# The sample's threshold search as a seventh column of the prompt's search, in a two-layer decoder trunk

## The reference, cut to what matters

```python
sc = indexer_scores(iqb, iwb, ik)                   # relu(iq . ik), weighted over 8 index heads
sc = jnp.where(adm[None], sc, -jnp.inf)             # only admissible keys
_, idx = lax.top_k(sc, topk)                        # topk = 256
valid = idx <= qpos[None, :, None]
return attend_selected(qb, k[bi, idx], v[bi, idx], valid)
```

## Time and profile before

| what | value |
|---|---|
| median of 3 runs | 2226.55 us (2226.4 to 2228.27) |
| time of the profiled execution | 2228.04 us |
| its span, first to last instruction | 2226.3 us |
| mean granted TensorE clock | 0.933 of full speed |
| busy: TensorE, VectorE, ScalarE, GpSimd | 2014.0, 1001.8, 685.4, 599.0 us |
| first Q unit's rotation starts | 1359.60 us |
| attention over the prompt starts on VectorE | 1580.09 us |
| the prompt's counts (L1394, 6 areas x 31 bits) | 175.9 us |

### The profile page before, as it was taken

How to read it: one execution, slowest core, us unless ns; L and a number is a source line. 1 busy time by engine, 2 the same in 40 slices (tenths; PEclk the granted TensorE clock), 3 DMA queues, 4 the chain that set the end, 5 groups by cost and what they waited for, 6 DMA issues and landing times. The chain is left out here.

```text
span 2226.3 us, 33761 instructions
## 1 busy us (share of the span) xinstructions
PE 2014.0 (90%) x12572; PEld 1815.4 (82%) x12572; DVE 1001.8 (45%) x1842; ACT 685.4 (31%) x929; POOL 599.0 (27%) x321
## 2 busy tenths in 40 slices
PE   7999998999999999996898788989878987879998
PEld 6999998999999999995853478989655655569898
DVE  3123333111234421425578667779889821230533
ACT  4243332122433322322464211222444522120310
POOL 4333333553334356352110011112101100025221
PEclk8999999999999999997988788989999987689999
DMA  5222222222222232211301202112300014341021
GB/s 166 76 67 77 74 75 75 66 85 85 77 84 84 85 85 79 77 35 49 117 12 35 67 20 78 28 48 95 99 1 1 1 36 152 121 148 47 29 69 40
DMA packets 240515, 152.87 MB, mean 69 GB/s; under 512 B 24946, under 2 KB 235634, under 8 KB 240050
## 3 DMA queue, kind: packets, MB, share of 16 engines
q1 hardware_dynamic: 229314, 140.74, 21.3%
q10 hardware_dynamic: 10192, 9.46, 1.3%
q0 software_dynamic: 928, 1.62, 0.3%
HBM read 135.33 MB, written 16.43 MB: 68 GB/s over the span
## 5 line engine op out<-in xcount | busy, mean ns | idle before, releaser
L392 POOL TENSOR_TENSOR wlo<-wraw,whi 128x1024 fp32r<-128x1024 f32 x177 | 430.1, 2430 | 951.6 <-ACT whi L387 949.9
L404 PE MATMUL PS<-hhi_g,whi 128*128 128x288 f32 (+1 forms) x1536 | 328.2, 295 | 14.4 <-POOL wlo L392 10.8
L404 PE MATMUL PS<-hhi_g,wlo 128*128 128x288 f32 (+1 forms) x1536 | 321.3, 291 | 0.0
L404 PE MATMUL PS<-hlo_g,whi 128*128 128x288 f32 (+1 forms) x1536 | 321.0, 291 | 0.0
L404 PE MATMUL PS<-hhi,whi 128*128 128x364 f32 x1176 | 275.2, 344 | 48.7 <-POOL wlo L392 13.9
L387 ACT ACTIVATE whi<-wraw 128x1024 fp32r<-128x1024 f32 x177 | 186.6, 1055 | 357.7 <-PE PS L404 311.6
L404 PE MATMUL PS<-hlo,whi 128*128 128x364 f32 x1176 | 268.0, 337 | 0.0
L404 PE MATMUL PS<-hhi,wlo 128*128 128x364 f32 x1176 | 265.9, 335 | 0.0
L404 PEld LDWEIGHTS PS<-hhi,whi 128*128 128x128 f32 x1176 | 211.6, 197 | 57.7 <-issue 35.5
L404 PEld LDWEIGHTS PS<-hhi_g,whi 128*128 128x128 f32 x1536 | 243.5, 191 | 17.8 <-issue 10.7
L404 PEld LDWEIGHTS PS<-hlo_g,whi 128*128 128x128 f32 x1536 | 245.1, 191 | 0.0
(11 more groups left out here) (331 smaller groups left out, 2773.3 us busy)
## 6 DMA issues: line engine op xcount, KB each, us to landing
wraw<-in_w_in_a_dram SPq DMA_DIRECT2D x96, 512.0 KB, 3.9
wraw<-in_w_out_a_dram SPq DMA_DIRECT2D x32, 512.0 KB, 4.1
wraw<-in_w_in_b_dram SPq DMA_DIRECT2D x25, 512.0 KB, 3.7
wraw<-in_w_pe_gate_dram SPq DMA_DIRECT2D x16, 512.0 KB, 4.1
kpg<-in_cache_k_dram SPq DMA_DIRECT2D x64, 128.0 KB, 2.0
vpg<-in_cache_v_dram SPq DMA_DIRECT2D x64, 128.0 KB, 2.0
xs<-xT SPq DMA_DIRECT2D x1, 4368.0 KB, 12.6
xT<-xs SPq DMA_DIRECT2D x1, 4368.0 KB, 13.3
```

The lines of the kernel that those rows point to most:

```text
L392: nc.gpsimd.tensor_tensor(wlo[par][:], wraw[par][:], whi[par][:].bitcast(F32), ALU.subtract).then_inc(w_lo, 1)
L404: mm = nc.tensor.matmul(o, w[par][:, k, :], r(k, c0, cn), start=first and i == 0 and n == 0, stop=last and i == KD - 1 and n == 2)
```

## The change

The sample's first 19 bits (JOINT = 31 - 8 - 4) are taken together with the prompt's, from the first Q unit on: eight in the Q units and eleven after them. A joint bit has seven areas and seven columns, on 128 rows; `count` takes its number of rows from each area, so the sample's count still runs on 64 rows. Four memsets give rows 64 to 127 of column 6 defined values. The sample's last 12 bits stay in attention, in iterations 32 to 43 (SIDE = 32), and its resolve parts move to iterations 44 to 51.

```diff
@@ -332,7 +332,8 @@
         xs_out, xs_in, tabI, tabQ, pt_in = (sem(n) for n in ("xs_out", "xs_in", "tabI", "tabQ", "pt_in"))
 
         BITS, EARLY_BITS, KV_BITS = 31, 8, 2 * NKV
-        SIDE = 25
+        JOINT = BITS - EARLY_BITS - KV_BITS
+        SIDE = 32
 
 
         iq = {n: sem(f"iq_{n}") for n in ("swa", "t1d", "add")}
@@ -1386,11 +1387,13 @@
 
             PROMPT = (P, slice(0, NBLK - 2), [sc[:, block_off(b):block_off(b + 1)] for b in range(2, NBLK)])
             SAMPLE = (NS, slice(NBLK - 2, NBLK - 1), [scs[:]])
+            BOTH = (P, slice(0, NBLK - 1), PROMPT[2] + SAMPLE[2])
 
             def count(group, op, against):
 
-                rows, cols, areas = group
+                _, cols, areas = group
                 for j, x in enumerate(areas, cols.start):
+                    rows = x.shape[0]
                     own.link(nc.vector.tensor_scalar(acc[0:rows, 0:x.shape[1]], x,
                                                      0.0 if against is None else against[0:rows, j:j + 1], None,
                                                      op, ALU.add, accum_out=cnt[0:rows, j:j + 1]))
@@ -1417,12 +1420,13 @@
                 own.link(nc.vector.tensor_tensor(tbit[r, c], tbit[r, c], mbit[r, c], ALU.bitwise_xor))
                 own.link(nc.vector.tensor_scalar(bitc[r, c], bitc[r, c], 1, None, ALU.logical_shift_right))
 
-            BIT_LINKS = 5 + len(PROMPT[2])
-
-            def search_bits(trips):
+            def bit_links(group):
+                return 5 + len(group[2])
+
+            def search_bits(group, trips):
                 with dve.Fori(0, trips) as i:
-                    own.enter(i, BIT_LINKS)
-                    search_bit(PROMPT)
+                    own.enter(i, bit_links(group))
+                    search_bit(group)
                 own.leave(trips)
 
 
@@ -1453,7 +1457,7 @@
 
             dve.wait_ge(sc_ok, NBLK - 2)
             start_search(PROMPT)
-            search_bits(EARLY_BITS)
+            search_bits(PROMPT, EARLY_BITS)
             dve.wait_ge(ss_["sum"], DEC_B)
             nc.vector.tensor_copy(scs[:], PSF[0:NS, 0:SLS]).then_inc(ss_["cp"], 1)
 
@@ -1480,19 +1484,21 @@
 
 
             dve.wait_ge(ss_["ok"], 1)
+            for t, fill in ((tbit, 0), (bitc, 0), (sgn, 1.0), (cnt, 0.0)):
+                own.link(nc.vector.memset(t[NS:P, NBLK - 2:NBLK - 1], fill))
             start_search(SAMPLE)
 
 
             dve.wait_ge(kk_["st"], 16 * 6)
             with dve.Fori(0, NH // 2) as i:
-                own.enter(i, 2 + 2 * BIT_LINKS)
+                own.enter(i, 2 + 2 * bit_links(BOTH))
                 for ff in range(2):
                     f = 2 * i + ff
                     rotate(qq, U_Q + f, f, (U_Q + ff) % 2, qT[:, bass.ds(f, 1), :].rearrange("p o n -> p (o n)"),
                            csQ, snQ, gqk[:, 0:1])
-                    search_bit(PROMPT)
+                    search_bit(BOTH)
             own.leave(NH // 2)
-            search_bits(BITS - EARLY_BITS - KV_BITS - NH)
+            search_bits(BOTH, JOINT - NH)
             for rows, j in ((NS, slice(0, 1)), (P, slice(1, 9))):
                 dve.wait_ge(qq["rt"], 2)
                 own.link(nc.vector.reciprocal(qs[0:rows, j, :], qs[0:rows, j, :]))
@@ -1562,10 +1568,10 @@
                         resolve(PROMPT, b - 2, sc[:, block_off(b):block_off(b + 1)], kTb[:, 0], kTb[:, 1], part)
                 if n == NH:
                     sample_operands()
-                if SIDE <= n < SIDE + BITS:
+                if SIDE <= n < SIDE + BITS - JOINT:
                     search_bit(SAMPLE)
-                elif n >= SIDE + BITS:
-                    resolve(SAMPLE, NBLK - 2, scs[:], Ps, acc, n - SIDE - BITS)
+                elif SIDE + BITS - JOINT <= n < SIDE + BITS - JOINT + 8:
+                    resolve(SAMPLE, NBLK - 2, scs[:], Ps, acc, n - SIDE - BITS + JOINT)
                 if n + 2 < len(STEPS):
                     mask_and_max(n + 2)
             inverse_sums(NGR - 1)
```

## The result

The changed kernel takes 2235.88 us (median of 5 runs, 2235.04 to 2239.62) against 2226.55 of the kernel before. The ratio is 1.0041 with a 95% interval of 1.0028 to 1.0053. The profiled execution took 2235.04 us with a span of 2233.3.

A forecast was written before the change was run, and what follows sets the result against it. VectorE's order was taken to bound the kernel ahead of attention, with VectorE and TensorE close bounds in attention. 26.2 - 10.3 - 6.0 = +9.9 us on the 2226.55 median gave 2236.4 us, range 2230.0 to 2243.0.

The forecast's parts named there:

- VectorE's order is the chain from the first Q unit to attention: Q and Z units: VectorE has no slack, arrives last at attention by some 2 us, so added counts delay attention fully.
- The term: Ahead of attention: 19 added sample counts of 1.38 us each, 26.2 us in all, range 22 to 30.
- The five small instructions with a seventh column and the memsets cost nothing: Joint bits and before the first tq: seventh column priced at nothing, four memsets hidden in 5.24 us of waiting.
- The Z units move by 9.7 us, and TensorE then stands idle some 20: Ahead of attention: Z units move 7 x 1.38 = 9.7 us, the last ends near 1584, TensorE idles some 20 us.
- First stretch: Attention iterations 26 to 31, which lose their bits: step 33's maximum at 1641.0 instead of 1651.29, 10.3 us gained.
- Second stretch: Attention iterations 32 to 43: twelve bits as before, VectorE bound, same pace, nothing gained or lost.
- Third stretch: Attention iterations 44 to 53, no bits: TensorE alone needs 36.5 us instead of 42.5, 6.0 us gained.
- The sum: Whole kernel: 26.2 - 10.3 - 6.0 = +9.9 us, 2236.4 us against the median.
- TensorE not the next bound: Rival, attention iterations 26 to 31 and 44 to 53: all 43.7 us come back, -17.5 us, 2209; chance 0.06.
- The counts hidden ahead of attention: Rival, Q rounds and Z units: slack on VectorE hides the joint counts, leaving -16.3 us, 2210; chance 0.04.
- Less coming back because of the clock: Rival, attention's third stretch: TensorE's clock at the lower level, stretch gives nothing, +15.9 us, 2242.5; chance 0.12.
- The count at the plain rate: Rival, joint bits: added counts run at the plain comparison's rate, 15.4 us added, -0.9 in sum, 2225.6; chance 0.02.

The follow-up runs named there:

- e4_joint_q: Changed kernel with 8 joint bits (Q units) instead of 19, the other 23 in attention iterations 32 to 54: 2230.53 us, ratio 1.0000 to the kernel before.
- e5_gap: Changed kernel with the Q units' 8 sample bits as separate bits in the wait for ScalarE's swap, 11 joint bits kept: 2225.73 us, ratio 0.9993.
- e9_balance: Changed kernel without joint bits or memsets: sample bits in VectorE's waits and attention, two prompt bits moved ahead of K and V: 2192.84 us, ratio 0.9826.
- e2_no_side: Changed kernel without the 12 sample bits of attention iterations 32 to 43, resolve parts kept: 2224.62 us, ratio 0.9979 to the kernel before.
- e1_two_counts: Changed kernel with the sample's count issued twice in each of its 19 joint bits: 2263.57 us, ratio 1.0139 to the kernel before.
- e8_plain: Changed kernel with the sample's count in the 19 joint bits as a plain comparison without accumulator: 2229.75 us, ratio 0.9992.

## Why the prediction was right, point by point

**VectorE's order is the chain from the first Q unit to attention.** Right, and shown by four runs: the added counts (+25.8 us), doubled (another +24.1), eleven of them taken out (e4_joint_q, -12.2) and eight (e5_gap, -10.0). The term was 26.2. The short instructions that the splits stretched took 6.3 us extra before and 5.5 after, so without that chance the term would have measured 26.6. The prediction's "by some 2 us" was too large a lead: it set the end of the last bit against attention's start, with six small instructions between them, and the first maximum also waits for the store of the last Z unit, which by the estimate at e9_balance had landed only some 0.85 us earlier. With work added to VectorE this changed nothing.

**The five small instructions with a seventh column and the memsets cost nothing.** In the Q rounds each of the five takes 0.15 or 0.17 us, on seven columns as on six, and the first tq still waits 4.41 us for TensorE behind the memsets, where it waited 5.24. A round grew by 1.46 us (10.21 over seven), 0.08 more than the 1.38 of a count; where these 0.6 us in all come from no run shows.

**The Z units move by 9.7 us, and TensorE then stands idle some 20.** The last Z unit came at 1583.60 (forecast near 1584), the idle time was 19.83 us.

**First stretch, -10.3.** Measured -10.8.

**Second stretch, no change.** 54.42 against 54.41 us: VectorE's pace, untouched.

**Third stretch, -6.0.** This term was mis-sized: it measured -7.3. TensorE needed 35.10 us from iteration 45 to 54, not 36.5, because the waits of 0.35 us in even iterations, which I had carried over from the stage with bits, are gone: in iteration 46 above the transposes follow 1.50 us after the logits began, and seven blocks of logits at 0.215 are 1.51. To attention's end the stretch gave 18.1 - 10.8 = 7.3.

**The sum.** 25.8 - 18.1 = +7.7 us in these two stages, against +9.9. The two measured ratios give 6 to 12 and 5 to 9 us. That the median came within 0.5 us of the forecast is luck: the return was 1.8 us larger than its term and the added part 0.4 smaller, and the rest of the program, which the change leaves alone, varies by more than that from one execution to the next.

**The rivals.** TensorE not the next bound: out by e2_no_side, where 27.6 us less of VectorE's work gave 13.6. The counts hidden ahead of attention: out by e1_two_counts. Less coming back because of the clock: the 20 us of idle time ahead of attention changed nothing, attention's first 5 us are at 0.50 (the 1.2 GHz level) in both kernels, and steps 0 to 26 keep their distances to within 0.5 us. The third stretch, where this rival saw the lower level, ran at 0.99 (1719.70 to 1760.00). The count at the plain rate: out. The existing counts run at 1337 ns, and e8_plain shows that it is the accumulator that makes the difference. The Trainium skill, "VectorE: DVE Perf Modes", section "The perf-mode tier table (the rule you actually need)", has fp32 tensor_scalar at two elements a cycle: the trace agrees for the plain form (779 ns) and not for the one with a sum (1337 ns).

## What to carry to other kernels

When work is moved out of a stage, price it twice: at what it costs where it goes (all of it, if that engine's own order is the chain there), and at what comes back where it leaves (only down to the next engine's time, here 18.1 of 43.7 us). Before widening an instruction chain that is already the critical one, look inside it for waits on another engine: a whole bit of 2.3 us fitted into a wait of 3.5 us and cost nothing, where one more column of 1.38 us cost all of itself. And among stages with two close bounds put movable work where the other engine's steps are longest, and not in every step.

## What the runs showed of the hardware that was not expected

A plain fp32 comparison on VectorE (64x1088) took 779 ns alone, and up to 2596 ns when GpSimd's subtraction of 128x1024 was running; the same pass with an accumulated sum took 1337 ns and was not held up in the kernel after or in e1_two_counts. The short instructions on six or seven columns were held up too: two to four times in the Z units, by 3.7 to 8.4 us in all. That chance meeting was most of the difference between expected and measured stages in e4_joint_q, e5_gap and e8_plain. The Trainium skill, "GPSIMD Engine Reference", section "1. Specifications", says that GpSimd's SBUF interfaces are shared with VectorE and that instructions in a two-port mode or with two SBUF inputs contend; the trace agrees for the plain comparison and for the small ones, most of which have two inputs (mbit, tbit, cand, thr); in the kernel before one with a single input (bitc) was held up as well, at 2.36 us.

The largest hold-up of this kind lies in the Q rounds and is in both kernels. The last add of a rotation reads two SBUF tiles, and in the round of e5_gap shown above it runs beside a split, while that of the eighth Q unit has none beside it:

```profile
1382.08 2.42 POOL L393 TENSOR_TENSOR wlo<-wraw,whi 128x1024 fp32r<-128x1024 f32 x1 [14.19 <-ACT whi L388]
1382.39 3.26 DVE L1321 TENSOR_TENSOR qT<-tq,swp 128x1092 f32 x1
...
1483.11 1.29 DVE L1321 TENSOR_TENSOR qT<-tq,swp 128x1092 f32 x1
```

The same add takes 3.26 us and 1.29 us, and the long one ends 1.15 us after the split. In the kernel before seven of the eight adds took 2.89 to 3.26 us and the eighth 1.30, in the kernel after 3.21 to 3.25 and 1.29. That is some 13 us on the very chain that the change made longer, more than the change cost. It leaves the price of the change as it is, since it stands on both sides, but the rotation's row of 3.2 us is not what that add takes by itself. No run moved the split, so what doing so would give back is open.
